# A hybrid decoder step on one core: the input projection in split operands, with x kept in DRAM meanwhile

## The reference, cut to what matters

```python
xn = rmsnorm(x, norm_mix)
proj = xn @ w_in                      # 2048 x 8448 with padding: 132 units of 128 x 1024
u, q, k, v, qi, ki, wi, gl = jnp.split(proj, ...)
q, k = rope(rmsnorm(q, q_norm), pos), rope(rmsnorm(k, k_norm), pos)
qi, ki = rope(qi, pos), rope(ki, pos)
y_att = attend(q, k, v, qi, ki, wi, pos)          # top-k by index scores, then attention
y_ssm, h_re, h_im = s5_scan(u, ...)               # complex recurrence over the positions
y_ssm = gelu(y_ssm); y_ssm = y_ssm * sigmoid(y_ssm @ w_glu)
merged = gates[0] * (y_ssm @ w_branch[0]) + gates[1] * (y_att @ w_branch[1])
x = x + merged @ w_out
x = x + (silu(gate) * up) @ w_ffn_down            # gate, up = split(rmsnorm(x) @ w_ffn_up)
```

## Time and profile before

| | us |
|---|---|
| median of 3 runs | 3351.09 (3347.22 to 3352.36) |
| profiled execution | 3350.28 |
| its span, first to last instruction | 3348.5 |
| TensorE busy | 3193.5 (95%) |
| TensorE weight loads busy | 2936.6 (88%) |
| VectorE busy | 1824.9 (54%) |
| ScalarE busy | 1072.5 (32%) |
| GpSimd busy | 312.8 (9%) |
| input projection and what is woven into it, layer 1 | 34.9 to 649.0 |

### The profile page before, as it was taken

The page is one execution under the profiler, slowest core; times in us unless marked ns, Lnnn a source line. Parts: engine busy times, 40 slices in busy tenths (PEclk is TensorE's granted clock), DMA queues, the critical chain, the costliest instruction groups (busy, mean ns, idle before and its releaser), DMA issues.

```text
span 3348.5 us, 58011 instructions
## 1 busy us (share of the span) xinstructions
PE 3193.5 (95%) x22528; PEld 2936.6 (88%) x22528; DVE 1824.9 (54%) x3184; ACT 1072.5 (32%) x1514; POOL 312.8 (9%) x264
## 2 busy tenths in 40 slices
PE   7999898999999999999989998889999999999998
PEld 5777766889999999999967787668899999999998
DVE  2135748658655545555421367496586555455553
ACT  1011031343454433333210110314434454333332
POOL 3230000143000000000032300001520000000000
PEclk9999999999999999999999999999999999999999
DMA  5443322555555555555344433225645555555553
GB/s 179 143 138 123 116 94 89 189 194 162 172 182 180 189 177 167 177 183 191 133 158 143 132 126 113 88 95 190 202 162 176 181 181 188 178 166 178 184 190 133
DMA packets 142221, 531.24 MB, mean 159 GB/s; under 512 B 19424, under 2 KB 20576, under 8 KB 141184
## 3 DMA queue, kind: packets, MB, share of 16 engines
q1 hardware_dynamic: 132512, 503.06, 45.2%
q0 software_dynamic: 9216, 25.18, 2.4%
q10 hardware_dynamic: 352, 1.11, 0.1%
HBM read 524.23 MB, written 5.05 MB: 158 GB/s over the span
## 4 chain that ended last, share of the span: by engine, by line
PE 43%; DVE 5%; issue 1%; ACT 1%; DMA 0%; POOL 0%; ACTq 0%; DVEq 0%; SPq 0%
PE main L853 8%; PE main L854 8%; PE main L855 8%; PE main L465 6%; PE main L628 4%; PE main L502 2%; PE main L489 2%; PE main L747 1%; PE main L749 1%; PE main L748 1%; DVE tmp L1313 1%; DVE merged_low L1462 1%; DVE tmp L1460 0%; DVE w_mid_low L1436 0%; DVE arena L1321 0%
## 5 line engine op out<-in xcount | busy, mean ns | idle before, releaser
L1529 DVE TENSOR_TENSOR w_ffn_low<-ring_ffn,w_ffn_high 128x1024 fp32r<-128x1024 f32 (+1 forms) x480 | 638.6, 1331 | 487.0 <-ACT w_ffn_high L1100 486.5
L853 PE MATMUL main<-x_ffn_high,w_ffn_high 128*128 128x264 f32 x2816 | 799.8, 284 | 2.5 <-issue 2.5
L854 PE MATMUL main<-x_ffn_low,w_ffn_high 128*128 128x264 f32 x2816 | 798.4, 284 | 0.0
L855 PE MATMUL main<-x_ffn_high,w_ffn_low 128*128 128x264 f32 x2816 | 798.1, 283 | 0.0
L1100 ACT ACTIVATE w_ffn_high<-ring_ffn 128x1024 fp32r<-128x1024 f32 (+1 forms) x480 | 548.2, 1143 | 723.9 <-PE main L855 720.9
L853 PEld LDWEIGHTS main<-x_ffn_high,w_ffn_high 128*128 128x128 f32 x2816 | 531.1, 189 | 3.3 <-issue 3.3
L854 PEld LDWEIGHTS main<-x_ffn_low,w_ffn_high 128*128 128x128 f32 x2816 | 531.5, 189 | 0.0
L855 PEld LDWEIGHTS main<-x_ffn_high,w_ffn_low 128*128 128x128 f32 x2816 | 528.6, 188 | 0.0
L465 PE MATMUL main<-xn,ring 128*128 128x264 f32 x1856 | 428.0, 393 | 11.9 <-DVE xn L1131 7.1
L465 PEld LDWEIGHTS main<-xn,ring 128*128 128x128 f32 x1856 | 358.7, 194 | 78.3 <-issue 15.4
L853 PE MATMUL main<-hidden_high,w_ffn_high 128*128 128x264 f32 x1408 | 402.7, 286 | 9.2 <-DVE hidden_low L1553 9.2
(11 more groups left out here) (328 smaller groups left out, 4175.0 us busy)
## 6 DMA issues: line engine op xcount, KB each, us to landing
ring_ffn<-in_w_up SPq DMA_DIRECT2D x352, 512.0 KB
ring<-in_w_in SPq DMA_DIRECT2D x264, 512.0 KB
ring_ffn<-in_w_down SPq DMA_DIRECT2D x128, 704.0 KB
ring<-in_w_br SPq DMA_DIRECT2D x64, 512.0 KB, 3.7
ring<-in_w_out SPq DMA_DIRECT2D x64, 512.0 KB, 3.7
ring<-in_w_glu SPq DMA_DIRECT2D x16, 512.0 KB, 5.1
x<-in_x SPq DMA_DIRECT2D x1, 2112.0 KB, 8.1
out_x<-x SPq DMA_DIRECT2D x1, 2112.0 KB, 6.4
```

Source lines behind the costliest of these rows:

```text
L853: mm(out, wfh[:, slot, w], high[:, kk, :], start=kk == 0, stop=False)
L854: mm(out, wfh[:, slot, w], low[:, kk, :], start=False, stop=False)
L855: m = mm(out, wfl[:, slot, w], high[:, kk, :], start=False, stop=kk == chunks * kts - 1)
L1529: tt(wfl[:, s, 0:cols], ring_ffn[:, s, 0:cols], wfh[:, s, 0:cols].bitcast(F32), ALU.subtract).then_inc(low_ready, 1)
```

## The change

The input projection is computed as the rest: `unit` with high and low parts of x and of the weights, 24 matmuls for 8 products. The high parts of w_in (130 a layer) go to ScalarE (`highs_to`), the first two to VectorE; low parts go by `LOW_DVE` to VectorE (0 to 3, the odd units of 5 to 55, 127, 129, 131) or else to GpSimd (4, the even ones of 6 to 54, 56 to 126, 128, 130). `xh` lies where x lay, so x is kept in DRAM: `o["x"]` gets x at the start and each layer's result in four stores during the last FFN phase, and 16 pieces are read back beside w_out's weights. The ring of the projection has six places and not four. The high parts have three or four places; a high part waits for the unit three (late: two) before it.

Also changed: b-bar and the sign of cc move from GpSimd to VectorE; the norms of queries and keys are summed into 12 rows of one bank (one-hot stationary), with one root, one reciprocal, and 12 matmuls that spread the result; units 88 and 89 come before the wait for `ties_counted`; GpSimd's last 16 key fetches are moved earlier; the loops over units are written out.

```diff
+PRE, LATE = 2, 104
+LOW_DVE = {0, 1, 2, 3} | set(range(5, 56, 2)) | {127, 129, 131} | set(range(G_GLU, G_BR1)) | set(range(G_OUT, G_END))
+SPLIT_DVE = {k for k in range(NT) if k % 3 == 0}
...
                 sp.dma_start(x[:], d["x"]).then_inc(consts_in, 16)
+                sp.dma_start(o["x"], d["x"]).then_inc(spilled, 16)
                 sp.dma_start(consts[:], d["consts"]).then_inc(consts_in, 16)
...
+                    for u in range(G_GLU, G_END):
+                        load(u)
+                        if X_AT <= u < X_AT + NT:
+                            k = u - X_AT
+                            sp.dma_start(x[:, k, :], o["x"][:, k, :]).then_inc(x_in, 16)
...
+                    def unit_part(u, seq, c, high, low, k0, n, opens, closes, made=None):
+                        if k0 == 0:
+                            if opens:
+                                pe.wait_ge(bank_free[seq % 4], seq // 4 + 1)
+                            if u in LOW_DVE:
+                                pe.wait_ge(low_dve, lows_of(True, u))
+                            else:
+                                pe.wait_ge(low_pool, lows_of(False, u))
...
+                            mm(out, wh[:, w], high[:, 8 * c + k, :], start=opens and k == 0, stop=False)
+                            mm(out, wh[:, w], low[:, 8 * c + k, :], start=False, stop=False)
+                            m = mm(out, wl[:, w], high[:, 8 * c + k, :], start=False, stop=closes and k == 7)
...
+                    for f in range(28, 44):
                         for c in range(2):
-                            slot = (2 * seq + c) % 4
...
+                            w_in_unit(f, c)
+                            pe.wait_ge(count_ready, 2 * (f - 28) + c + 1)
                             mm(side[0][:, 0:1], same_seq, n_over, start=True, stop=True).then_inc(total_ready, 1)
...
+                    for t in range(NHK):
...
+                        mm(side[0][0:NHK, 0:T], one_hot[:, NHK - 1 - t:2 * NHK - 1 - t], sq[:, t % 2, :],
+                           start=t == 0, stop=t == NHK - 1).then_inc(qsum_ready, 1)
...
+                    for t in range(NHK):
...
+                        mm(side[t % 4][:, 0:T], ident[0:NHK, t:t + 1].to_broadcast([NHK, P]), rs[0:NHK, 0, :],
+                           start=True, stop=True).then_inc(qinv_spread, 1)
...
+                    def highs_to(last):
...
+                            act.wait_ge(u_in[u % 6], 16 * (u // 6 + 1))
+                            if high_free(u):
+                                act.wait_ge(units, high_free(u))
...
+                            af(high, raw, ACT.Copy).then_inc(unit_high, 1)
...
+                    for k in range(NT + 2):
+                        if k < NT:
+                            stt(xn[:, k, :], x[:, k, :], gn[:, 0, k:k + 1], rs[:, 0, :], ALU.mult, ALU.mult).then_inc(xn_ready, 1)
+                        if k >= 2:
+                            x_low(k - 2)
...
+                    def lows_to(last):
+
+                        nonlocal next_low
+                        while next_low <= last:
+                            u = next_low
+                            next_low += 1
+                            if u in LOW_DVE:
+                                continue
+                            raw, high, low = unit_w(u)
+                            pool.wait_ge(unit_high, u + 1 - PRE)
+                            g.tensor_tensor(low, raw, high.bitcast(F32), ALU.subtract).then_inc(low_pool, 1)
...
+                    for n in range(32):
+                        pool.wait_ge(units, max(1, n - 2))
+                        lows_to(max(1, n - 2) + 3)
                         fetch_keys(n)
```

More of the change, by code:

```diff
@@ L436, in _ @@
                             for s, freed in enumerate((67, 69, 70, 72)):
-                                sp.wait_ge(units, UN_GLU + freed)
+                                sp.wait_ge(units, G_GLU + freed)
                                 load_ffn(src, s, s, cols)
+                        if not up and half == 1:
+                            for n in range(count):
+                                sp.wait_ge(low_ready, n0 + n - 3)
+                                load_ffn(src, half * count + n, n % 4, cols)
+                                if n % 8 == 7 and n >= 15:
+                                    store_x(n // 8 - 1)
+                            store_x(3)
+                            continue
                         with sp.Fori(1 if n0 == 0 else 0, count // 4) as i:
@@ L479, in w_in_blocks @@
-                    def w_in_blocks(first, count):
-                        blocks(first, count, 2 * first, 2, 8, lambda k: xn[:, k, :])
-                    def w_in_unit(first, c):
-                        u = 2 * first + c
-                        if c == 0:
-                            pe.wait_ge(bank_free[first % 4], first // 4 + 1)
-                        pe.wait_ge(w_in[u % 4], (u // 4 + 1) * 16)
-                        for k in range(8):
-                            m = mm(main[first % 4][:, 0:T], ring[:, u % 4, k * P:(k + 1) * P], xn[:, 8 * c + k, :],
-                                   start=c == 0 and k == 0, stop=c == 1 and k == 7)
-                        m.then_inc(units, 1)
@@ new lines, in unit, with w_in_unit, w_in_blocks @@
+                    def unit(u, seq, c, high, low, opens=True, closes=True, made=None):
+                        unit_part(u, seq, c, high, low, 0, 8, opens, closes, made)
+                    def w_in_unit(f, c, made=None):
+                        unit(2 * f + c, f, c, xh, xl, c == 0, c == 1, made)
+                    def w_in_blocks(first, count):
+                        for f in range(first, first + count):
+                            for c in range(2):
+                                w_in_unit(f, c)
@@ L974, in bu @@
                         for v in range(2 * HALF):
+                            if v % 8 == 0 and not (half and v == 24):
+                                highs_to((55 if half == 0 else 103) + v // 8)
                             act.wait_ge(bu_ready, 32 * half + v + 1)
@@ L1601, in _, with lows_to @@
-                    pool.wait_ge(c_in, 16)
-                    g.tensor_scalar(cc[:, 1], cc[:, 1], -1.0, None, ALU.mult).then_inc(cneg, 1)
-                    for n in range(8, 32):
-                        pool.wait_ge(units, 2 + n)
-                        fetch_keys(n)
+                    next_low = 0
+                    def lows_to(last):
+                        nonlocal next_low
+                        while next_low <= last:
+                            u = next_low
+                            next_low += 1
+                            if u in LOW_DVE:
+                                continue
+                            raw, high, low = unit_w(u)
+                            pool.wait_ge(unit_high, u + 1 - PRE)
+                            g.tensor_tensor(low, raw, high.bitcast(F32), ALU.subtract).then_inc(low_pool, 1)
```

552 lines of the change are left out of this document (302 added, 250 removed).

## The result

The kernel after takes 3492.72 us, median of 4 runs (3491.78 to 3494.02), where before took 3351.09 (3347.22 to 3352.36): ratio 1.0425, 95% interval 1.0407 to 1.0443. It is 4.2% slower. The profiled execution has a span of 3490.9 us against 3348.5, a difference of 142.4.

What follows compares the result with a forecast made beforehand. TensorE bounds most stages, with VectorE nearly full in counting and attention. Two layers of +52 +40 -22 give +140, plus +9 once: 3350.3 + 149 = 3499, said as 3500 us; range 3390 to 3590.

Steps and rivals of the forecast that it cites:

- counting: 32 units beside the first scan: turns go from 3.78 to 5.4 us, +52 us a layer, between +33 and +64.
- attention and second scan: 22 units: some 20 low parts of 2.25 us less VectorE's idle, +40 us a layer, between +22 and +45.
- x's parts: Start of each layer: products 0 and 1 wait for x's split, +10 us a layer, between +3 and +13.
- A unit takes 2.93 us: Input projection where TensorE sets the pace: 24 matmuls take 2.93 us against 3.59 in fp32, saving about 0.64 a unit.
- VectorE's two-input instructions and GpSimd's low parts take turns: Both scan stages: the two engines alternate whole instructions, costing +52 and +40 us a layer.
- The first rival: Scan stages: the engines don't shut each other out, -47 us a layer, 3265 us in all; chance 0.13.
- Phases that fall well: Rival: engines take turns, but both scan stages fall at their lower ends (+33, +22), 3360 to 3430 us; chance 0.10.
- The clock: Rival: TensorE's clock falls as well, being at work 3.1 of 5.4 us in the counting stage; chance 0.12.
- The copy at the start: x's DRAM-to-DRAM copy stands ahead of the constants: +9 us once, between 0 and +12.
- Units 2 to 19: VectorE's odd low parts stand behind its other work and GpSimd's low parts: +9 us a layer, between 0 and +13.
- Rotations, index scores: Index-head rotation and index scores: low parts delay accumulations and a two-buffer ring, +9 us a layer, between 0 and +14.
- Picks and norms: New query and key norms: -3 us a layer, between -7 and +3; two units in the last-turn wait: 0.

Runs made afterwards that it cites:

- experiment 12: Kernel after without the low parts of units 4 to 19 of each layer, third product reading the high part instead: ratio 1.0351 to the kernel before.
- experiments 1 to 3: Kernel before plus 54 idle GpSimd operations a layer in counting and attention: subtractions, ratio 1.0341; writes, 1.0014; copies, 1.0350.
- experiment 4: Kernel after without the low parts of units 56 to 125, third product reading the high part instead: ratio 0.9743 to the kernel before.
- experiments 7 to 9: Kernel after, counting's GpSimd low parts released by the count: 1.0472; ahead of the search step: 1.0434; the latter with a per-partition scalar in that step: 1.0394.
- experiment 7: Kernel after with each GpSimd low part of the counting released by the count, one a turn: ratio 1.0472 to the kernel before.
- experiment 5: Kernel after with the low parts of units 56 to 125 moved from GpSimd to VectorE: ratio 1.0106 to the kernel before.
- experiment 2: Kernel before plus 54 idle GpSimd writes of zeros to 128x2048 a layer, in counting and attention: ratio 1.0014.
- experiment 11: Kernel before with the change's new query and key norms and its order of TensorE's work around the picks: ratio 0.9953.
- experiment 1: Kernel before plus 54 idle GpSimd subtractions of a 128x1024 piece from itself a layer, in counting and attention: ratio 1.0341.

## Why the prediction was right

The forecast of 3500 us was right in the time (3492.7) and in what sets it. The terms (us; a layer, layer 1):

| term | predicted | measured |
|---|---|---|
| copy of x, once | +9 | +5.8 |
| counting | +52 (32 turns of 5.4) | +51.7 (31 turns of 5.46) |
| attention and second scan | +40 | +40.8 |
| x's parts and the first 20 units | +10 + 9 - 12.8 = +6.2 | +8.4 |
| units 20 to 55 | -23.0 + 9 = -14.0 | -23.7 |
| picks and norms, 12 units | -7.7 - 3 + 0 = -10.7 | -4.4 |
| the other 10 units | -6.4 + 3 = -3.4 | -0.3 |
| GLU to output projection | 0 | -3.4 |
| sum of the last five | -22 | -23.4 |

- *A unit takes 2.93 us.* 2.91 in experiment 12. Right.
- *VectorE's two-input instructions and GpSimd's low parts take turns.* Right in place and size, and shown: experiments 1 to 3 make a loss of this kind out of idle work, experiment 4 takes it away, and in experiments 7 to 9 a turn is the sum of both engines' work less 0.3 to 0.8 us. The turns are 0.06 us longer than taken and one fewer, which evens out. The first rival, no exclusion, forecast 3265 us. That is what the kernel without the 70 low parts has (0.9743 of 3351 is 3265; against the kernel before, its counting is 14.6 us shorter where the rival said 12, and its attention 1.6 longer where the rival said 0), so its sum was good and its premise false.
- *Phases that fall well.* This rival stood on the turn's lower end of 4.8 us, +33. Three phases gave 5.41, 5.46 and 5.62 in the mean. None was mild: in each that was tried a two-input instruction of VectorE stood within 0.3 us of the low part's start. With the one at the search step removed a turn is 5.13.
- *The clock.* It fell, from 1.00 and 0.99 to means of 0.82 and 0.86 in the two scan stages. No run shows the clock's case that the range took in, the clock so low that TensorE sets the turn: the counting turns took 5.46 us at 0.82, and the longest, of experiment 7, 5.62 at 0.87. It is 1.00 in the counting when the low parts are gone (experiment 4) or on VectorE (5). TensorE is busy 125 of 169 us in the one, 101 of 103 and 106 of 134 in the others. It didn't set the time of these two stages: VectorE was busy for 161 of 169 us, and for 139.5 of 146. After the last count it may have cost the 2.8 us named in experiment 4.
- *The copy at the start.* The range 0 to 12 held it. The price was taken from the bytes at 230 GB/s, one transfer behind the other. The two ran beside each other: x took 8.4 us from issue to landing, and 8.1 before. The last number is that time (us), in the kernel after, then before:

```profile
x<-in_x SPq DMA_DIRECT2D x1, 2112.0 KB, 8.4
out_x<-in_x SPq DMA_DIRECT2D x1, 2112.0 KB, 13.5
...
x<-in_x SPq DMA_DIRECT2D x1, 2112.0 KB, 8.1
```

- *Units 2 to 19.* The way is the predicted one, a low part of VectorE's that stands behind its other work (a wait of 8.9 us), but the low parts cost 13.9 there, above the bound of 13 that the prediction gave. What is left for x's parts is 7.3 (8.4 + 12.8 - 13.9) and not 10; 2 us remain between the sums.
- *Rotations, index scores.* Mis-sized: 9 us of delays were expected in units 20 to 55, and the whole saving of a unit came through (-23.7 for 36 units at 0.64). GpSimd's key fetches were moved in the same change; whether that took the delays away wasn't tried.
- *Picks and norms.* Mis-sized. The prediction let the new order around the picks and the blocking of the last scan turns cancel, 0 together. The order is worth 7.9 us (75.7 to 67.8), and the low parts of that stage cost 12.6 (73.2 against 60.6), 4.7 together. The norms gave 1.9 (77.6 to 75.7) and not 3.
- *The rest.* The other 10 units gave next to nothing. The stretch from the first part of y to the first FFN input, which the prediction left at 0, got 3.4 us shorter; no run shows why.

The near match of the last line is thus partly luck: -9.7 and -3.4 against +6.3, +2.2 and +3.1. The two big terms are not: each came within 1 us, by the mechanism that was predicted.

## What to carry to other kernels

Work that reads SBUF and is given to GpSimd "beside" VectorE is to be priced as VectorE's own wherever VectorE runs instructions with two tensor inputs from SBUF, at GpSimd's duration, which was twice VectorE's here (a low part of 128x1024 in the kernel after: 2.41 us and 1.22 by the median); work that only writes is not (0.14% in experiment 2). Before cheaper products are paid for with elementwise work, look at which engine bounds each stage: where TensorE waits at a scan's pace already, 0.64 us less a unit is not worth 1.22 more on VectorE. And two independent units in a known wait of 10 us brought 0.4%, where the whole change lost 4.2%.

One version was not tried: split operands outside units 56 to 125, plain fp32 inside. From the rows above an estimate is -15.3 us a layer up to the first count, -9.8 after the last one (experiment 11's order and norms) and -4.8 after the attention, twice, and +5.8 for the copy: some 54 us or 1.6% less than before.

## What the runs showed of the hardware that was not expected

- An instruction of one column (0.16 us) waits as long as a wide one for a GpSimd read of 128x1024: it took 1.48 to 2.12 us in the rows above, and one of 512 columns 2.40 and 2.84 where it takes 0.69 alone. A short instruction is not a small risk.
- A GpSimd copy of 128x2048 takes 1.97 us (median) and excludes; a write of the same 128x2048 takes 1.80 us and doesn't.
- The same subtraction of 128x1024 took 1.89 us at the least into fp32 (experiment 1) and 2.34 into fp32r (the kernel after), but the first read one input twice; which of the two makes the difference wasn't tried.
- How the low parts fall against the scan hardly mattered in the three phases tried: 5.41 to 5.62 us a turn, in bursts of three or one by one.
- TensorE waits in both, but the granted clock of the counting was 0.82 with turns of 5.46 us and 1.00 with turns of 4.33 (experiment 5). In the kernel before it was 0.63 in the 10.4 us of wait for the last scan turns, and 1.00 there with two units in that wait (experiment 11).
